# The decay products of a forward state-space sweep: float32 triangles against two float32r parts made by ScalarE and GpSimd

## The reference, cut to what matters

```python
acs = jnp.cumsum((dt * a).reshape(b, nc, CHUNK, g, r), axis=2)
seg = acs[:, :, :, None] - acs[:, :, None, :]
decay = jnp.exp(jnp.where(lower, seg, -jnp.inf))
cb = jnp.einsum('bctgn,bcsgn->bctsg', cc, bc)
y_diag = jnp.einsum('bctsgr,bcsgrp->bctgrp', cb[..., None] * decay, xdt)
```

## Time and profile before

| | |
|---|---|
| time, median of 3 runs | 3135.67 us (3130.63 to 3136.36) |
| profiled execution, span | 3142.7 us (the page states no other time for it) |
| PE busy | 2889.9 us, 92% of the span |
| DVE busy | 1590.2 us, 51% |
| POOL busy | 971.2 us, 31% |
| ACT busy | 617.9 us, 20% |
| mean granted TensorE clock | 0.939 of full speed |
| forward sweep, from the first D0 to the last output add | about 1962.8 to 2138.2 us of the span |

### The profile page before, as it was taken

One profiled execution on the slowest core, in us unless ns is written; L12 is line 12 of the kernel. 1 busy time (PEld: TensorE's weight loads), 2 busy tenths in 40 slices (PEclk: granted clock), 3 DMA queues, 4 the chain that ended last, 5 costly groups with the idle time before them and its releaser, 6 DMA issues. The chain is left out here.

```text
span 3142.7 us, 33928 instructions
## 1 busy us (share of the span) xinstructions
PE 2889.9 (92%) x13390; PEld 2355.7 (75%) x13390; DVE 1590.2 (51%) x2008; ACT 617.9 (20%) x991; POOL 971.2 (31%) x515
## 2 busy tenths in 40 slices
PE   5988986999999999996987898888999999999997
PEld 5777775788888888885875676556887788888885
DVE  8575552375444433366654795675246422222247
ACT  3212213231111000022222001553112101111101
POOL 2121120445333333351212233001254533333343
PEclk8898998999999999996988899999998999999998
DMA  3211113232222222232001143113132211111122
GB/s 139 60 53 58 53 52 141 68 95 84 83 73 73 67 67 68 79 101 90 27 27 33 59 129 121 61 54 147 47 108 94 74 50 51 47 47 47 47 70 98
DMA packets 89065, 231.04 MB, mean 74 GB/s; under 512 B 27584, under 2 KB 30784, under 8 KB 88960
## 3 DMA queue, kind: packets, MB, share of 16 engines
q1 hardware_dynamic: 52528, 173.72, 16.9%
q10 hardware_dynamic: 36432, 55.88, 5.6%
HBM read 199.02 MB, written 29.36 MB: 73 GB/s over the span
## 5 line engine op out<-in xcount | busy, mean ns | idle before, releaser
L193 POOL CAST w_hi<-w_raw 128x1024 fp32r<-128x1024 f32 x254 | 279.4, 1100 | 2109.1 <-PE ps L206 2096.6
L202 PE MATMUL ps<-a_hi,w_hi 128*128 128x512 f32 x2080 | 704.7, 405 | 46.2 <-PEq L2517 18.8
L195 POOL TENSOR_TENSOR w_lo<-w_raw,w_hi 128x1024 fp32r<-128x1024 f32 x254 | 688.7, 2711 | 20.3
L204 PE MATMUL ps<-a_lo,w_hi 128*128 128x512 f32 x2080 | 688.4, 397 | 0.0
L206 PE MATMUL ps<-a_hi,w_lo 128*128 128x512 f32 x2080 | 686.6, 396 | 0.0
L202 PEld LDWEIGHTS ps<-a_hi,w_hi 128*128 128x128 f32 x2080 | 398.8, 194 | 134.2 <-issue 29.1
L204 PEld LDWEIGHTS ps<-a_lo,w_hi 128*128 128x128 f32 x2080 | 401.1, 193 | 85.3
L206 PEld LDWEIGHTS ps<-a_hi,w_lo 128*128 128x128 f32 x2080 | 399.5, 192 | 86.3
L204 PE MATMUL ps<-g_b,w_hi 128*128 128x512 f32 x1216 | 413.9, 396 | 0.0
L202 PE MATMUL ps<-g_b,w_hi 128*128 128x512 f32 x1088 | 366.9, 399 | 30.1 <-DVE g_b L1239 20.7
L206 PE MATMUL ps<-g_b,w_lo 128*128 128x512 f32 x1088 | 362.2, 395 | 0.0
(11 more groups left out here) (402 smaller groups left out, 3059.2 us busy)
## 6 DMA issues: line engine op xcount, KB each, us to landing
w_raw<-in_wstream SPq DMA_DIRECT2D x254, 512.0 KB, 3.5
ada_w<-in_ada_w ACTq DMA_DIRECT2D x50, 512.0 KB, 3.6
y_by_token<-y ACTq DMA_DIRECT2D x12, 512.0 KB, 3.0
tmp_b<-mixer_out SPq DMA_DIRECT2D x8, 512.0 KB, 3.3
x_res_b<-in_xT SPq DMA_DIRECT2D x2, 2048.0 KB, 12.9
x_block<-x_res_b SPq DMA_DIRECT2D x16, 256.0 KB, 3.2
z_rows<-ada_w ACTq DMA_DIRECT2D x8, 512.0 KB, 2.7
u_rows<-pad ACTq DMA_DIRECT2D x8, 512.0 KB, 4.8
```

The source lines that it names most:

```text
L193: pool.tensor_copy(k.w_hi[:, s, :], k.w_raw[:, s, :]).then_inc(k.w_high, 1)
L195: pool.tensor_tensor(k.w_lo[:, s, :], k.w_raw[:, s, :], k.w_hi[:, s, :].bitcast(F32), ALU.subtract).then_inc(k.w_split, 1)
L202: pe.matmul(o, w_hi, a_hi[:, c], start=first, stop=False)
L204: pe.matmul(o, w_hi, a_lo[:, c], start=False, stop=False)
```

## The change

The steps are written as float32r instead of float32 and are then called the high part; the two strict triangles are copied to float32r once (`tri`). A low part is added: `dta_lo` is `dta` minus its float32r value (`dta_hi`, made by one ScalarE and one VectorE instruction), and GpSimd scales the same triangles by it, 32 instructions of 128x128 for each chunk, into four new tiles `steps_lo`. TensorE multiplies both parts, so that a group has eight float32r products where it had four float32 ones. It waits for the high part and then for the low part. GpSimd starts with the first chunk once the last large product of the phase has read `a_lo` (`tile_done`), and with group `g` of the next chunk once D0 or D1 of this chunk is done. Three of the four tiles are new SBUF allocations, for which the scratch space of software-made DMAs is set to 1024 bytes.

```diff
+        low_places = [over("low5_00", 2 * KT - 3, F32R)] + [sb(f"low5_{j}", [P, SEQ], F32R) for j in range(3)]
+        steps_lo = [low_places[0:2], low_places[2:4]]
+        tri = sb("tri5", [P, 2, P], F32R)
+        dta_hi, dta_lo = sb("dta_hi5", [P, NC, 32], F32R), sb("dta_lo5", [P, NC, 32])
@@ gpsimd
+            pool.wait_ge(s["dta_split"], 1)
+            pool.wait_ge(k.tile_done, UZ_END)
+            for i in range(NC):
+                for g, j in enumerate((D0, D1)):
+                    if i:
+                        pool.wait_ge(s["x_done"], fwd + J * (i - 1) + j + 1)
+                    for r in range(2):
+                        for h in range(HPG):
+                            at = SSM_HEADS * r + HPG * g + h
+                            ins = pool.tensor_scalar(steps_lo[r][g][:, h * P:(h + 1) * P],
+                                                     k.mats[:, (TRI_LE, TRI_GE)[r], :], dta_lo[:, i, at:at + 1], None,
+                                                     ALU.mult)
+                        ins.then_inc(s["lows_ready"], 1)
@@ tensor
                     for r in range(2):
                         for h in range(2):
-                            ins = pe.matmul(X[j % 2][:, h, :], k.mats[:, (TRI_GT, TRI_LT)[r], :], steps[r][g][:, half_of(h)],
-                                            start=r == 0, stop=r == 1)
+                            pe.matmul(X[j % 2][:, h, :], tri[:, r, :], steps[r][g][:, half_of(h)], start=r == 0, stop=False)
+                    pe.wait_ge(s["lows_ready"], 4 * i + 2 * g + 2)
+                    for r in range(2):
+                        for h in range(2):
+                            ins = pe.matmul(X[j % 2][:, h, :], tri[:, r, :], steps_lo[r][g][:, half_of(h)],
+                                            start=False, stop=r == 1)
                     ins.then_inc(s["x_done"], 1)
@@ scalar
+            act.activation(dta_hi[:, :, :], v.dta[:, 0:NC, :], ACT.Copy).then_inc(s["dta_high"], 1)
...
+            act.activation(tri[:, 0, :], k.mats[:, TRI_GT, :], ACT.Copy)
+            act.activation(tri[:, 1, :], k.mats[:, TRI_LT, :], ACT.Copy)
             make_steps(0, 0)
@@ vector
             dve.wait_ge(s["pooled"], KT)
+            dve.wait_ge(s["dta_high"], 1)
+            tt(dta_lo[:, :, :], v.dta[:, 0:NC, :], dta_hi[:, :, :].bitcast(F32), ALU.subtract).then_inc(s["dta_split"], 1)
@@ kernel
-    nc = bacc.Bacc("TRN2", target_bir_lowering=False, num_devices=1)
+    nc = bacc.Bacc("TRN2", target_bir_lowering=False, num_devices=1, dynamic_dma_scratch_size=1024)
```

More of the change, by code:

```diff
@@ L1972, in sb, with over @@
             return ctx.enter_context(nc.sbuf_tensor(n, shape, dt))
-        def over(n, tile):
-            return nc.alloc_sbuf_tensor_at(n, [P, SEQ], F32, offset=k.a_at + tile * SEQ * 4)
+        def over(n, tile, dt=F32):
+            return nc.alloc_sbuf_tensor_at(n, [P, SEQ], dt, offset=k.a_at + tile * SEQ * 4)
         state, y_even, xw = (sb(n, [P, SEQ]) for n in ("state5", "y5", "xw5"))
@@ L1995, in phase5 @@
         y_odd = over("y_odd5", KT - 3)[:, :]
-        steps = [[over(f"steps5_{r}{g}", KT * r + KT - 2 + g) for g in range(NGRP)] for r in range(2)]
+        steps = [[over(f"steps5_{r}{g}", KT * r + KT - 2 + g, F32R) for g in range(NGRP)] for r in range(2)]
+        low_places = [over("low5_00", 2 * KT - 3, F32R)] + [sb(f"low5_{j}", [P, SEQ], F32R) for j in range(3)]
+        steps_lo = [low_places[0:2], low_places[2:4]]
+        tri = sb("tri5", [P, 2, P], F32R)
+        dta_hi, dta_lo = sb("dta_hi5", [P, NC, 32], F32R), sb("dta_lo5", [P, NC, 32])
         xdt = [spare[:, 0:SEQ], spare[:, SEQ:2 * SEQ]]
@@ L1999, in phase5 @@
         stage = k.ada_w
-        s = signals(nc, ctx, "p5", "chain xw_ready xdt_ready steps_ready off_added w_ready y_ready y_back y_out0 y_out1 y_in0 y_in1 z_out d_out first_state "
+        s = signals(nc, ctx, "p5", "chain xw_ready xdt_ready steps_ready lows_ready dta_high dta_split off_added w_ready y_ready y_back y_out0 y_out1 y_in0 y_in1 z_out d_out first_state "
                                    "d_in dhi dlo x_done x_free0 x_free1 cleared area_in pooled")
```

## The result

| | before | changed |
|---|---|---|
| time, median | 3136.02 us (4 runs) | 3167.54 us (4 runs, 3161.59 to 3178.78) |
| ratio to before | | 1.0111, 95% interval 1.0079 to 1.0144 |
| profiled span | 3142.7 us | 3167.1 us |
| sweep, first D0 to the end of the last output add | 175.4 us | 217.1 us |
| chunk, output add to output add | 23.4, 21.7, 20.55 us | 27.3, 26.7, 25.0 us |

What follows compares the result with a forecast made beforehand. The forward sweep was taken as bound by a chain holding D0 and D1, with no busy engine. 20.6 us gained less 4.5 for turns gave 16 us off 3135.7, so 3120 us; own range 3111 to 3127, 8 in 10 up to 3165.

Steps and rivals of the forecast that it cites:

- What bounds the kernel: Forward sweep: a chain and no busy engine; D0 and D1, 7.13 us of products, stand wholly on it.
- TensorE's part: D0 and D1: a group takes 1.8 us instead of 3.42, DIAG starts earlier in every chunk; 20.6 us gained.
- The price of a low part: One GpSimd TENSOR_SCALAR of 128 columns, taken as 0.25 us from the CAST's row; 32 a chunk just fit.
- The upper bound: Price of one low part from above, by the two-input TENSOR_TENSOR's 2.2 ns an element: 0.38 us.
- VectorE and GpSimd take turns: Whole instructions exclude each other; five VectorE instructions on the chain wait half a low part each, 4.5 us in all.
- The rival that came true: GpSimd becomes the bound, TensorE waiting for low parts in D0 or D1; slower, 3143 to 3192 us; chance 0.33.
- the prediction's own row for 0.6: Case of the GpSimd-bound rival with a low part of 0.6 us: a time of 3192 us.
- The clock rival: Chunks 3, 6 and 7 can get a half-speed stretch too, 1.7 us each; 3125 to 3128 us; chance 0.07.
- DIAG may meet one: TensorE's DIAG may also fall into a half-speed stretch, though it was never hit before; no separate size.
- The small parts: Triangle copies and `dta` split ahead of the first chunk cost under 1 us; ScalarE's 32 steps stay at 9.45 us.
- The ISA row: GpSimd, ahead of the first TENSOR_SCALAR: comes once and is covered before the first chunk's D0.
- the prediction's balance: GpSimd's 32 lows plus VectorE's two-input instructions against a chunk: decides at 0.35 us a low (half-speed chunks), 0.30 (others).

Runs made afterwards that it cites:

- copy run: Changed kernel with GpSimd's 32 scalings a chunk replaced by plain 128-column copies to float32r, scaled triangles left out; one run, 3116.31 us, sweep 154.0 us.
- low-parts-once run: Changed kernel with GpSimd making only chunk 0's low parts, which TensorE multiplies in every chunk; ratio 0.9982 to before, median 3116.26 us.
- the second job: The changed kernel itself measured once more, four runs; ratio 1.0150 to before.
- TENSOR_TENSOR run: Changed kernel with the same low parts made by four 1024-column GpSimd TENSOR_TENSORs a chunk; ratio 1.0160 to before, sweep 206.4 us.
- wide run: Changed kernel with four 1024-column TENSOR_SCALARs a chunk, all eight heads taking the first one's scalar; one run, 3121.62 us, sweep 164.5 us.

## Why the prediction was wrong

- *What bounds the kernel, and TensorE's part (20.6 us):* right, as far as one trace of each kernel tells. The copy run shortened the sweep by 21.4 us (chunk 0 gained 2.8 where 2.7 was worked out), the low-parts-once run its seven intervals by 20.
- *The price of a low part:* this is the step that failed: "the CAST is the nearest row; for the scalar I add a little and take 0.25", with 0.38 from above. It measured 0.60, so that 32 of them are 19.2 us a chunk instead of 8, where the prediction itself had 7.4 to 8.3 us left for them. The CAST was well enough priced (0.22 worked out, 0.29 measured), but the TENSOR_SCALAR does not follow it: 2.5 ns a column though it reads one tensor, and a fixed part of 0.28 us, for which the one-element MEMSET's 0.10 stood in. The upper bound joined the dearest slope to the cheapest fixed part, and so was none.
- *VectorE and GpSimd take turns:* right for GpSimd in direction, which stood behind VectorE for 8.1 us a chunk, where 12.2 were charged. It takes both terms to make the loss: by this count 19.2 us alone would still have fitted into a chunk of 20.5, 27.3 did not. Wrong for VectorE: I charged five of its instructions half a low part each, 4.5 us in all, and beside the TENSOR_SCALARs its two-input instructions grew by 0.03 us on average (the weights by 0.05, the longest to 1.40 us). In the copy run these 4.5 us did not show either. The rule cited from the Trainium skill's "SBUF — State Buffer", section "SBUF: two separate sides", that the loser is blocked for the whole instruction, agrees with VectorE beside TENSOR_TENSORs (2.80 to 2.91 us instead of 1.22) and not with VectorE beside TENSOR_SCALARs.
- *The rival that came true* (0.33): its place, the wait for the low part, holds, and GpSimd is the bound. Its rule, 32 low parts plus 12.2 us, does not hold in size: with the undisturbed 0.60 it gives 31.4 us a chunk, and the prediction's own row for 0.6 gives 3192 us; measured were 27.3 us and 3167.5 (3176.4 in the second job). The range to 3165 was reached with a low part of 0.48; that the time lies only 2.5 us above it is two errors in part cancelling, a price too low and turns too dear. Not in it was chunk 0: its 32 low parts were taken as covered, and it lost 10 us.
- *The clock rival:* chunks 6 and 7 kept the full clock in D0 and D1 in the low-parts-once run, as forecast; chunk 3 got a half-speed stretch there, and chunk 5 lost its own. "DIAG may meet one" came true elsewhere: in seven of eight chunks of the TENSOR_TENSOR run, 6.1 us in the chunk taken apart, and in two of the wide run.
- *The small parts:* under 1 us was allowed, 0.2 us came (12.3 instead of 12.1 us from the last large product to D0). ScalarE's 32 steps take 9.45 us as before. The ISA row ahead of the first TENSOR_SCALAR had no visible cost; the instruction that follows the last TENSOR_TENSOR (1936.12 + 2.34 in the trace) starts at 1938.52.

## What to carry to other kernels

Neighbouring rows give an instruction that no row shows an estimate, but no upper bound: 0.38 us was called one and 0.60 came. Ask what price the plan can bear (0.30 to 0.35 here by the prediction's balance) and how near the estimate lies to it, with the count of short instructions as the multiplier. When work moves to an idle engine, compare its whole amount in a period with the period, the time that it stands behind other engines included: here 19.2 us of its own and 8.1 of standing could not fit in 20, 16 instead of 32 instructions did, and the rest found room on ScalarE. Then most of the TensorE saving that was there all along arrives (12 to 13 us of the time, 16 to 18 of the sweep). And where a run comes out slower than its balance, look at the granted clock of each job before putting the rest down to contention: in the TENSOR_TENSOR run a hold-up of 2 us was followed by 6 us of half speed.

## What the runs showed of the hardware

- GpSimd, float32 in and float32r out, undisturbed: CAST 0.288 us for 128 columns and 1.04 for 1024; TENSOR_SCALAR 0.60 with a scalar per partition, 0.53 with a constant, 2.84 for 1024 columns. ScalarE does the same scaling of 128 columns every 0.295 us.
- A VectorE instruction with two SBUF inputs took 2.8 to 2.9 us instead of 1.22 beside GpSimd TENSOR_TENSORs of 1024 columns, 1.22 to 2.06 beside TENSOR_SCALARs of as many columns, and at most 1.40 beside TENSOR_SCALARs or CASTs of 128. In turn a TENSOR_SCALAR of 0.60 us took 1.33 beside one such instruction and up to 2.6 in a row of them, and 0.60 beside a VectorE instruction that reads PSUM.
- A VectorE COPY of 1024 float32 columns took 2.60 us beside 128-column CASTs, 0.70 to 0.89 beside 128-column TENSOR_SCALARs with a scalar per partition, and 0.69 before.
- In the changed kernel TensorE waited 4.5 us or more in each chunk; the granted clock over the sweep was 0.81, before it was 0.95, and the products right behind the wait ran at half speed (ST at 0.57).
